# Gate and up products of a routed expert layer: one 128-column weight block, or two 64-column tiles

## The chip, the cores and the metric

The kernel runs on one core of a Trainium2 chip. The core has a matrix engine (TensorE, called PE in the profile), a vector engine (DVE), a scalar engine (ACT), GpSimd (POOL), a queue engine (SP), and sixteen DMA engines that bring data from main memory. The metric is the device time of one execution in microseconds; the median of three runs stands for a kernel. The profile lists a matmul twice: the loading of the stationary operand into the array (LDWEIGHTS, in the rows called PEld) and the streaming of the moving operand through it (MATMUL, called PE).

## The reference

The program is one step of a two-layer network on 640 tokens (128 prompt and 512 sample tokens) of width 1024. Layer 0 mixes the tokens by a bidirectional mLSTM, layer 1 by a bidirectional gated DeltaNet. After each mixer comes a mixture of 16 experts in which the experts choose tokens, and this is the part that is changed:

```python
aff = jax.nn.softmax((x @ w_router).astype(jnp.float32), -1)
gsel, idx = lax.top_k(jnp.swapaxes(aff, 1, 2), cap)
xs = x[bidx, idx]
hdn = jax.nn.silu(jnp.einsum('becd,edf->becf', xs, w_gate)) * jnp.einsum('becd,edf->becf', xs, w_up)
out = jnp.einsum('becf,efd->becd', hdn, w_down) * gsel[..., None].astype(x.dtype)
return jnp.zeros_like(x).at[bidx, idx].add(out)
```

Each expert takes 64 sample tokens and 16 prompt tokens, 80 in all. Its gate, up and down weights are 1024 by 1024 numbers each, in float32: 12 MB for one expert, of which there are 32 in the two layers.

## The kernel before

The work of each engine is written out by hand in program order, and semaphores tie the engines together; no planner decides anything. PE goes through the two layers one after the other: the modulation vectors, the projections, the scan of the mixer, the output projection (`mixer_tail`), and then `experts`.

An expert `e` has six weight halves of 2 MB, held in six slots: two halves each of gate, up and down, every half being 1024 rows by 512 columns. In the slots a row index is split into 8 blocks of 128 (`kt`) that lie on the 128 partitions. The loads of the next expert into a slot start when PE has finished the slot's products of the current expert: PE increments `moe_used`, SP (line 334) or ACT (line 681) waits for that and issues the load, and PE waits on `land[j]` for it before it uses the slot again.

On PE an expert has three stages. `hidden` (lines 1196 to 1206) forms the gate and up products. For each of the four halves `j` it goes through four blocks of 128 output features (`fb`) and for each through the eight blocks of the contraction (`kt`): the stationary operand is a 128 by 128 block of the weights, the moving operand is the block `kt` of the expert's tokens, 80 columns (`xsT`). The result, 128 features by 80 tokens, is accumulated over `kt` in bank `j` of PSUM at columns `fb*80`. That is 4 x 4 x 8 = 128 matmuls. `turn` (line 1193) transposes the tokens of the next expert, with eight matmuls. `down` (line 1215) has the 80 hidden columns as the stationary operand and 512 columns of the weights as the moving operand, 16 matmuls.

The operands are float32, and the trace holds two passes, each with a load and a streaming, for a float32 matmul of the program (a transpose has one). So an expert's 128 matmuls of `hidden` stand as 256 LDWEIGHTS and 256 MATMUL in the rows, its 16 of `down` as 32. "A pass" in this text is one load with its streaming.

ACT evaluates a tanh on the gate bank (line 687), and DVE makes the hidden values out of it (lines 1745 and 1748); `down` waits for the second half of these. DVE also scales and shifts the tokens of the next expert after the transposes, GpSimd gathers them and adds the finished rows of an expert to the output in memory. Expert 0, 1, 14 and 15 are written out, the others run in a loop whose body has two experts.

In the scan of layer 1 there is a place that the prediction reads too: lines 1088 and 1103 are matmuls of a 64 by 64 stationary block on one half of the partitions with 64 moving columns, which write to one half of the PSUM partitions.

Of the kernel before, what the change touches and what calls it, by code (L numbers as in the profile page):

```python
# [24 lines left out]
P = 128  # L25
D = 1024
KT = D // P
# [6 lines left out]
CAP = CAPS + CAPP  # L34
# [19 lines left out]
def backbone(nc, a):  # L54
# [3 lines left out]
    def S(name):  # L58
        if name not in sems:
            sems[name] = ctx.enter_context(nc.semaphore(name))  # L60
        return sems[name]
# [11 lines left out]
    with ctx:  # L73
        PS = ctx.enter_context(nc.psum_tensor("ps", [P, 8, HC], F32))
# [13 lines left out]
        slot = [s.rearrange("p (k n) -> p k n", k=KT) for s in SL]  # L88
# [48 lines left out]
        xsT = [wk[:, q * 640:(q + 1) * 640].rearrange("p (k c) -> p k c", k=KT) for q in range(2)]  # L137
# [55 lines left out]
        def moe_base(L, j):  # L193

            return ((L + 1) * sum(mix_slot(k) == j for k in range(MIX)) if j < 3 else 0) + L * EX
# [537 lines left out]
        def _(pe):  # L733
            mm = nc.tensor.matmul
# [433 lines left out]
            def gate_rows(first, bank, sem):  # L1168

                for c in range(2):  # L1170
                    for j in range(2):
                        for b in range(4):
                            ins = mm(PS[:, bank + 2 * c + j, b * P:(b + 1) * P],
                                     modT[:, first + 4 * j + b, c:c + 1].broadcast_to([P, P]), ident, start=True, stop=True)
                        ins.then_inc(sem, 1)

            def experts(L):
                pe.wait_ge(S("aff"), L * PER["aff"] + 1)
                tr(PS[0:EX, 2, 0:P], aff[:, 0, :], ident)
                for t in range(1, NT):  # L1180
                    ins = tr(PS[0:EX, 1, (t - 1) * P:t * P], aff[:, t, :], ident)
                ins.then_inc(S("afft"), 1)
                pe.wait_ge(S("topk"), L * PER["topk"] + 1)
                tr(PS[0:CAP, 3, 0:EX], vals[:, :], ident[0:EX, 0:EX])
                tr(PS[0:CAP, 3, EX:2 * EX], idf[:, :], ident[0:EX, 0:EX]).then_inc(S("selt"), 1)
                pe.wait_ge(S("sel"), L * PER["sel"] + 2)

                def turn(e, q, first):
                    pe.wait_ge(S("gathered"), L * PER["gathered"] + e * 16 + 16)
                    if not first:  # L1190
                        pe.wait_ge(S("xs_in"), L * PER["xs_in"] + e)
                    for kt in range(KT):
                        ins = tr(PS[:, 6 + kt // 4, (kt % 4) * CAP:(kt % 4 + 1) * CAP], xs[q][0:CAP, kt * P:(kt + 1) * P], ident[0:CAP, 0:CAP])
                    ins.then_inc(S("xs_turned"), 1)

                def hidden(e, q, first):
                    pe.wait_ge(S("xs_in"), L * PER["xs_in"] + e + 1)
                    for j in range(4):
                        pe.wait_ge(land[j], e * 16 + (16 * moe_base(L, j) + 16))
                        if not first:  # L1200
                            pe.wait_ge(S("hidden"), L * PER["hidden"] + e * 2 + (j // 2 - 1))
                        for fb in range(4):
                            for kt in range(KT):
                                ins = mm(PS[:, j, fb * CAP:(fb + 1) * CAP], slot[j][:, kt, fb * P:(fb + 1) * P],  # L1204
                                         xsT[q][:, kt, :], start=(kt == 0), stop=(kt == KT - 1))
                        ins.then_inc(S("moe_used"), 1)

                def down(e, q, first):
                    pe.wait_ge(S("hidden"), L * PER["hidden"] + e * 2 + 2)
                    for j in range(2):  # L1210
                        pe.wait_ge(land[4 + j], e * 16 + (16 * moe_base(L, 4 + j) + 16))
                        if not first:
                            pe.wait_ge(S("o_ready"), L * PER["o_ready"] + e * 2 + (j - 1))
                        for ft in range(KT):
                            ins = mm(PS[0:CAP, 4 + j, :], hdT[:, ft, :], slot[4 + j][:, ft, :],  # L1215
                                     start=(ft == 0), stop=(ft == KT - 1))
                        ins.then_inc(S("moe_used"), 1)

                def keep_clock(n):


                    for _ in range(n):
                        mm(PS[:, 4, :], ident, hT[:, 0, 0:HC], start=True, stop=True)

                keep_clock(5)
                turn(0, 0, True)
                keep_clock(3)
                hidden(0, 0, True)
                turn(1, 1, False)
                down(0, 0, True)  # L1230
                hidden(1, 1, False)
                turn(2, 0, False)
                down(1, 1, False)
                with pe.Fori(1, EX // 2 - 1) as i:
                    for q in range(2):
                        e = i * 2 + q
                        hidden(e, q, False)
                        turn(i * 2 + (q + 1), 1 - q, False)
                        down(e, q, False)
                hidden(EX - 2, 0, False)  # L1240
                turn(EX - 1, 1, False)
                down(EX - 2, 0, False)
                hidden(EX - 1, 1, False)
                down(EX - 1, 1, False)
                pe.wait_ge(S("hidden"), L * PER["hidden"] + 2 * EX)
                gate_rows(40, 0, S("g2b"))
# [601 lines left out]
```

## Time and profile before

| | |
|---|---|
| time, median of 3 runs (lowest to highest) | 3254.94 us (3253.11 to 3256.28) |
| span of the profiled execution, first to last instruction | 3254.3 us |
| PE busy with streaming, over the span | 3039.7 us (93%) |
| PE busy with weight loads (PEld) | 2229.6 us (69%) |
| DVE, ACT, POOL busy | 963.2, 577.3, 96.0 us |
| moved by DMA | 545.50 MB |

The profiled execution has no time of its own beside its span; the median of the runs is 0.64 us above the span. Durations of single instructions in the rows are longer than their distance from one to the next, because loads and streamings are pipelined: what a pass costs in a long row of them is the length of the group, less the duration of its last instruction, divided by the number of steps. All times below are in us from the span's start, unless they are marked ns.

### The profile page before, as it was taken

How to read it: one execution, taken by the hardware profiler on the slowest of the kernel's cores; microseconds unless marked ns; L12 is line 12 of the kernel's file. 1: busy time of each engine (PE TensorE's matmuls, PEld its weight loads, DVE VectorE, ACT ScalarE, POOL GpSimd, SP SyncE). 2: the span in 40 equal slices, each digit the busy share in tenths (PEclk: the TensorE clock that was granted, in tenths of full speed). 3: DMA queues.
4: the chain of work that ended last, by engine and by line, in shares of the span. 5: the costliest groups of instructions: out<-in, count | busy, mean ns of one | idle time of the engine just before them, and what ended most of it. 6: DMA issues, size and time to landing. Idle time of an engine off the chain costs nothing.

```text
span 3254.3 us, 43264 instructions
## 1 busy us (share of the span) xinstructions
PE 3039.7 (93%) x18405; PEld 2229.6 (69%) x18405; DVE 963.2 (30%) x2408; ACT 577.3 (18%) x1297; POOL 96.0 (3%) x145
## 2 busy tenths in 40 slices
PE   6999999797999999997999989999986999999994
PEld 1465479745887777771456459999944888777773
DVE  1100136643001000102177536666645010001002
ACT  3100111240000000003167212222242000000002
POOL 0000000000000000000000000000000000000000
PEclk9899998897999999998999999999997999999997
DMA  8411100217999999957411100000016899999992
GB/s 281 154 52 52 45 1 1 65 62 270 312 311 303 303 309 308 306 183 271 155 52 52 39 0 1 1 2 1 1 65 224 279 314 304 307 305 307 306 310 87
DMA packets 276365, 545.50 MB, mean 168 GB/s; under 512 B 15233, under 2 KB 23817, under 8 KB 276233
## 3 DMA queue, kind: packets, MB, share of 16 engines
q1 hardware_dynamic: 175049, 328.64, 29.4%
q10 hardware_dynamic: 93600, 188.75, 16.6%
q0 software_dynamic: 7584, 26.22, 3.2%
q8 instruction: 99, 1.62, 0.2%
q14 instruction: 33, 0.27, 0.0%
HBM read 517.89 MB, written 25.70 MB: 167 GB/s over the span
## 4 chain that ended last, share of the span: by engine, by line
PE 88%; DVE 6%; ACT 3%; DMA 2%; issue 1%; SPq 0%; DVEq 0%; POOL 0%; ACTq 0%
PE ps L1204 28%; PE ps L1215 14%; PE ps L803 8%; PE ps L813 6%; PE ps L760 5%; PE ps L1139 3%; PE ps L1101 3%; PE ps L804 2%; PE ps L1083 2%; PE ps L880 1%; PE ps L1115 1%; PE ps L791 1%; PE ps L950 1%; PE ps L966 1%; ACT L424 1%; ACT L423 1%
## 5 line engine op out<-in xcount | busy, mean ns | idle before, releaser
L1204 PEld LDWEIGHTS ps<-wk,slots 128*128 128x128 f32 x6144 | 691.1, 192 | 16.5 <-issue 16.0
L1204 PE MATMUL ps<-wk,slots 128*128 128x80 f32 x6144 | 689.9, 275 | 0.0
L1215 PE MATMUL ps<-qkv,og 128*80 128x512 f32 x1024 | 446.7, 594 | 2.4 <-DVE og L1748 1.3
L1215 PEld LDWEIGHTS ps<-qkv,og 128*80 128x80 f32 x1024 | 151.0, 150 | 275.5 <-issue 268.0
L803 PE MATMUL ps<-hT,slots 128*128 128x512 f32 x640 | 334.0, 604 | 3.1 <-ACT hT L455 3.1
L1204 PE MATMUL ps<-wk,qkv 128*128 128x80 f32 x2048 | 233.9, 275 | 0.0
L1204 PEld LDWEIGHTS ps<-wk,qkv 128*128 128x128 f32 x2048 | 231.3, 192 | 0.0
L804 PEld LDWEIGHTS ps<-hT,slots 128*128 128x128 f32 x640 | 123.5, 193 | 156.6 <-issue 156.6
L813 PE MATMUL ps<-slots,hT 128*128 128x512 f32 x480 | 209.3, 596 | 0.0
L760 PE MATMUL ps<-slots,cnd 128*2 128x512 f32 x384 | 172.0, 602 | 35.1 <-DVE x L1776 24.1
L1724 DVE COPY idc<-idT 80x1 uint32 (+1 forms) x32 | 4.8, 149 | 612.8 <-DMA moe_d<-og,idc 612.7
L813 PEld LDWEIGHTS ps<-slots,hT 128*128 128x128 f32 x480 | 91.8, 192 | 111.9 <-issue 111.6
L693 ACT ACTIVATE og<-ps,gsc 80x512 f32<-80x512 f32 x64 | 43.7, 683 | 657.8 <-PE ps L1215 657.8
L687 ACT ACTIVATE wk<-ps 128x320 f32<-128x320 f32 x64 | 28.0, 437 | 717.8 <-PE ps L1204 717.8
L1139 PE MATMUL ps<-slots,qkv 128*128 128x512 f32 x320 | 141.2, 600 | 8.0 <-DMA slots<-in_w_out_dram 5.7
L760 PEld LDWEIGHTS ps<-slots,cnd 128*2 128x2 f32 x384 | 31.2, 86 | 156.2 <-issue 155.8
L1748 DVE SCALAR_TENSOR_TENSOR og<-wk,ps 128x320 f32<-128x320 f32 x64 | 31.2, 487 | 327.1 <-PE ps L1204 327.1
L804 PE MATMUL ps<-hT,slots 128*128 128x128 f32 x640 | 124.1, 276 | 0.0
L1139 PEld LDWEIGHTS ps<-slots,qkv 128*128 128x128 f32 x320 | 60.8, 193 | 81.5 <-issue 81.5
L1745 DVE SCALAR_TENSOR_TENSOR wk<-wk,ps 128x320 f32<-128x320 f32 x64 | 31.2, 487 | 284.1 <-ACT wk L687 284.1
L1486 DVE SCALAR_TENSOR_TENSOR wk<-wk,vecT 128x128 f32<-128x128 f32 x192 | 105.9, 552 | 6.8
L803 PEld LDWEIGHTS ps<-hT,slots 128*128 128x128 f32 x640 | 99.9, 195 | 4.0 <-ACT hT L455 3.5
(261 smaller groups left out, 3228.5 us busy)
## 6 DMA issues: line engine op xcount, KB each, us to landing
slots<-in_w_gate_dram ACTq DMA_DIRECT2D x60, 2048.0 KB, 9.2
qkv<-in_w_down_dram SPq DMA_DIRECT2D x34, 2048.0 KB, 9.8
slots<-in_w_up_dram SPq DMA_DIRECT2D x32, 2048.0 KB, 10.2
qkv<-in_w_up_dram SPq DMA_DIRECT2D x32, 2048.0 KB, 7.8
qkv<-in_w_down_dram ACTq DMA_DIRECT2D x30, 2048.0 KB, 7.8
slots<-in_w_ada_dram SPq DMA_DIRECT2D x24, 2048.0 KB, 8.1
slots<-in_w_in_dram SPq DMA_DIRECT2D x16, 2048.0 KB, 8.1
slots<-in_w_out_dram SPq DMA_DIRECT2D x4, 2048.0 KB, 16.2
```

Source lines behind the costliest of these rows:

```text
L423: link(A(dst, src, ACT.Ln, scale=scale, bias=epst[:, 0:1]))
L693: A(osb[q][0:CAP, hf * HC:(hf + 1) * HC], PS[0:CAP, 4 + hf, :], ACT.Copy, scale=gsc[q][0:CAP, :]).then_inc(S("o_ready"), 1)
L760: ins = mm(PS[0:2, n % 2, :], cnd[:, 1, kt:16:8], slot[j][:, kt, :], start=(kt == 0), stop=(kt == KT - 1))
L803: mm(PS[:, b, :], w, hT[:, kt, P:TOK], start=(kt == 0), stop=(kt == KT - 1))
L804: ins = mm(PS[:, b + 1, 0:P], w, hT[:, kt, 0:P], start=(kt == 0), stop=(kt == KT - 1))
L813: ins = mm(PS[:, 2 * (i % n), :], hT[:, kt, t * P:(t + 1) * P], slot[sl][:, kt, :], start=(kt == 0), stop=(kt == KT - 1))
L1083: ins = mm(pack(four(PS[:, bx, :])[:, :, 0:64], l)[:, h], B["CM"][l % 2][:, h, :], cols1(B["D"][:, h, :], l, d), start=True, stop=True)
L1101: ins = mm(hb(2 * p + l % 2, h, 64), B["DT"][:, h, :], B["X"][:, h, :], start=True, stop=True)
L1139: ins = mm(PS[:, 6 + j, :], yT[:, kt, t * P:(t + 1) * P], slot[j][:, kt, :], start=(kt == 0), stop=(kt == KT - 1))
L1204: ins = mm(PS[:, j, fb * CAP:(fb + 1) * CAP], slot[j][:, kt, fb * P:(fb + 1) * P], xsT[q][:, kt, :], start=(kt == 0), stop=(kt == KT - 1))
L1215: ins = mm(PS[0:CAP, 4 + j, :], hdT[:, ft, :], slot[4 + j][:, ft, :], start=(ft == 0), stop=(ft == KT - 1))
L1486: ins = V.scalar_tensor_tensor(o_, s, w, o_, ALU.mult, ALU.add)
```

## The change

The innermost matmul of `hidden` becomes two. Each takes 64 of the 128 columns of the same weight block, streams the same 80 token columns, and writes its own half of the PSUM partitions, 0 to 63 or 64 to 127, at the same columns of the same bank. The two follow each other inside the loop over `kt`, so neighbouring matmuls alternate between the two halves of the array's columns. The results lie where they lay before; the number of matmuls in `hidden` goes from 128 to 256 for one expert, and from 4096 to 8192 for the program. The semaphore is incremented by the last of them, as before. On PE the order of the stages stays, and on the other engines no instruction is changed.

```diff
                         for fb in range(4):
                             for kt in range(KT):
-                                ins = mm(PS[:, j, fb * CAP:(fb + 1) * CAP], slot[j][:, kt, fb * P:(fb + 1) * P],
-                                         xsT[q][:, kt, :], start=(kt == 0), stop=(kt == KT - 1))
+                                for s in range(2):
+                                    c = fb * P + 64 * s
+                                    ins = mm(PS[64 * s:64 * s + 64, j, fb * CAP:(fb + 1) * CAP], slot[j][:, kt, c:c + 64],
+                                             xsT[q][:, kt, :], start=(kt == 0), stop=(kt == KT - 1))
                         ins.then_inc(S("moe_used"), 1)
```

## Rows read from the trace of the kernel before

**Rows 1.** The page: chain that ended last, and costliest groups (busy us, mean ns).

```profile
PE 88%; DVE 6%; ACT 3%; DMA 2%; issue 1%; SPq 0%; DVEq 0%; POOL 0%; ACTq 0%
PE ps L1204 28%; PE ps L1215 14%; PE ps L803 8%; PE ps L813 6%; PE ps L760 5%; PE ps L1139 3%; PE ps L1101 3%; PE ps L804 2%; PE ps L1083 2%; PE ps L880 1%; PE ps L1115 1%; PE ps L791 1%; PE ps L950 1%; PE ps L966 1%; ACT L424 1%; ACT L423 1%
...
L1204 PEld LDWEIGHTS ps<-wk,slots 128*128 128x128 f32 x6144 | 691.1, 192 | 16.5 <-issue 16.0
L1204 PE MATMUL ps<-wk,slots 128*128 128x80 f32 x6144 | 689.9, 275 | 0.0
...
L1204 PE MATMUL ps<-wk,qkv 128*128 128x80 f32 x2048 | 233.9, 275 | 0.0
L1204 PEld LDWEIGHTS ps<-wk,qkv 128*128 128x128 f32 x2048 | 231.3, 192 | 0.0
```

**Rows 2.** The chain in order of time, one expert of layer 0: start, length, what.

```profile
1019.77 0.56 PE ps L1193 x8
1020.33 0.03 issue
1020.35 13.96 PE ps L1215 x32
1034.31 28.54 PE ps L1204 x256
```

**Rows 3.** Timeline, 128-column loads: start, length, engine, line, shapes, count [idle before].

```profile
3015.80 7.23 PEld L1204 LDWEIGHTS ps<-wk,qkv 128*128 128x128 f32 x64
...
721.72 3.65 PEld L1145 LDWEIGHTS ps<-wrt,hT 128*128 128x128 f32 x32
```

**Rows 4.** Timeline, PE and PEld around the 64-column matmuls of layer 1.

```profile
1972.53 1.14 PE L1088 MATMUL ps<-slots 64*64 64x64 f32 x16
1973.60 0.65 PE L1006 MATMUL ps<-c,qkv 128*128 128x128 f32 x4
1974.09 1.06 PE L1008 MATMUL ps<-qkv 128*128 128x128 f32 x8
1975.08 1.14 PE L1103 MATMUL ps<-slots,wk 64*64 64x64 f32 x16
...
1975.08 1.00 PEld L1103 LDWEIGHTS ps<-slots,wk 64*64 64x64 f32 x16
```

**Rows 5.** Durations of these loads and streamings (min/median/max ns).

```profile
L1103 PEld LDWEIGHTS ps<-slots,wk x160: 129/135/135, 1975.1 to 2357.1; 64*64 64x64 f32 x160
L1103 PE MATMUL ps<-slots,wk x160: 218/218/267, 1975.1 to 2357.2; 64*64 64x64 f32 x160
L1193 PE MATMUL ps<-c,og x256: 230/232/236, 772.3 to 3152.7; 80*128 80x80 f32 x128
```

**Rows 6.** Timeline, streaming of 80 columns in the transposes, and the loads beside it.

```profile
1019.61 0.72 PE L1193 MATMUL ps<-c,og 80*128 80x80 f32 x8
...
1019.50 0.67 PEld L1193 LDWEIGHTS ps<-c,og 80*128 80x128 f32 x8
```

**Rows 7.** Windows: length, busy of PE, PEld, DVE, ACT, POOL, granted clock, DMA share, GB/s.

```profile
781.00:1441.00 660.00, 659.44 (x4563) 523.65 (x4563) 61.93 (x180) 34.05 (x61) 40.15 (x58) 1.00 0.89 301
1000.00:1043.07 43.07, 43.04 (x299) 33.99 (x297) 4.10 (x12) 2.24 (x4) 2.75 (x4) 1.00 0.91 307
740.00:760.00 20.00, 2.40 (x11) 1.56 (x10) 16.32 (x40) 0.27 (x1) 0.00 (x0) 0.50 1.05 387
```

## The prediction

> **What bounds the kernel now.** I read the page first: its chain puts 88% of the span on PE, and the line that changes, 1204, alone holds 28%; the groups give it 8192 loads and as many streamings, busy 922 us (691.1 and 231.3) and 924 us [rows 1]. The chain in order of time then shows a whole expert: 0.56 us of transposes, 13.96 of `down` and 28.54 of `hidden`, 43.07 us in all, with 0.03 us that is not PE [rows 2]. So inside an expert nothing but PE ends last, and each nanosecond on a pass of line 1204 is 8192 ns in the time. The windows say how far the next resource is: in such an expert the DMA share is 0.91 at 307 GB/s, and with PE nearly idle ahead of the experts it reached 387 GB/s [rows 7].
>
> What sets the pace of `hidden`? 64 loads of 128 columns take 7.23 us, so one follows another after (7.23 - 0.192) / 63 = 0.1117 us [rows 1, 3]. The router's matmuls load blocks of the same size and stream 16 columns instead of 80; theirs come every (3.65 - 0.19) / 31 = 0.1116 us [rows 3]. The distance doesn't depend on what is streamed, so the load sets it. The 80-column streaming can be read where the load is shorter, in the transposes: (0.72 - 0.232) / 7 = 0.0697 us [rows 5, 6]. A pass of line 1204 is thus a 112 ns load with a 70 ns streaming beneath it, and about 42 ns in which the array waits for weights.
>
> **The change, part by part.** It removes 8192 passes with a load of 128 columns and adds 16384 with a load of 64. Nothing else is added: no wait, no DMA, no instruction on DVE, ACT, POOL or SP.
>
> A 64-column load: the nearest rows are the 64 by 64 matmuls of line 1103, 16 loads in 1.00 us, (1.00 - 0.135) / 15 = 57.7 ns [rows 4, 5]. The row's rounding allows 57.3 to 58.0. They stream 64 columns, in less than that. That is a little over half of 112: 2 x 57.7 = 115.4 against 111.7 ns. So if loads go one after another and set the pace, splitting costs 115.4 - 111.7 = 3.7 ns for each old pass, up to 4.3 with the rounding: 8192 x 3.7 to 4.3 ns = 30 to 35 us. I take the upper end, 58.0 ns a load, since a group's length also carries a short first step.
>
> The streaming: two halves of 80 columns each, 2 x 69.7 = 139.4 ns for each old pass if they too go one after another. This is more than the two loads; PE would be bound by streaming, at 139.4 - 111.7 = 27.7 ns more for each old pass, 8192 x 27.7 = 227 us. If the halves of the array can stream at the same time, the streaming stays hidden. No row of this kernel shows neighbouring matmuls in different column halves: the sixteen passes of line 1103 all go to the same half, one after another.
>
> Between these two there is a middle case. A float32 matmul is two passes, so the order is two passes to the lower half, two to the upper. If a load has to wait until the stream ahead of it has begun, as in one undivided array, then of every two passes one shows its stream and one its load: 57.7 + 69.7 = 127.4 ns for each old pass, 15.7 more, 129 us.
>
> And from the other side: if both the loads and the streams of the two halves run side by side, an old pass costs one 80-column stream, 69.7 ns. `hidden` goes from 28.54 to 256 x 0.0697 = 17.8 us, and an expert's PE work to 17.8 + 0.56 + 13.96 = 32.4 us. Then DMA ends last: 43.07 us at 307 GB/s are 13.2 MB [rows 7], which take 34.2 us at 387 GB/s, or 43.07 x 0.91 / 1.05 = 37.3 us by the shares. 32 experts x (43.07 - 34.2 to 37.3) is a gain of 185 to 284 us.
>
> So the unknown runs from about -284 to +227 us, and the sign hangs on whether two weight loads go in parallel. Every row shows loads strictly one behind another on PEld, and the 128-column load is already as fast for its columns as the 64-column one. I take the loads as serial. For streams I take overlap between the halves: they use separate columns and separate PSUM partitions, and what a half waits for is only its own weights. That sets 116 ns, the value nearest to the rows of lines 1204 and 1103.
>
> The Trainium skill, page TensorEngine Tiling (Array Packing), section Tiling Modes, Key Properties, says that different tiles can execute weight loads and matmuls in parallel. No run here shows two tiles in turn, so the trace neither bears it out nor denies it; by this rule taken whole, the time would be that of the first rival.
>
> The switch of shape. Where 128-column matmuls are followed by 64-column ones, the first load is not pulled ahead. The last stream of line 1008 starts at 1974.09 + 1.06 - 0.275 = 1974.875 (its duration taken as line 1204's 275 ns [rows 1]), and line 1103 starts at 1975.08, 205 ns later, where the eight passes before stood (1.06 - 0.275) / 7 = 112 ns apart [rows 4]. On the way out, line 1088's last stream starts at 1972.53 + 1.14 - 0.218 = 1973.452 and line 1006 at 1973.60, 148 ns later instead of 58 [rows 4, 5]. That is 93 + 90 ns, and the first pass after it has its load uncovered, some 50 ns each. The new `hidden` is entered and left once for each expert: 32 x (93 + 90 + 2 x 40 to 50) ns = 8 to 9 us. It may be nothing, if a 64-column tile on all 128 rows needs no switch.
>
> The sum: 35 + 8 = 43 us on the chain, 3254.3 + 43 = 3297.3 for the span; the median of the runs stands 0.64 above the span now, so 3298. Nothing is late next: slots come free some 1.3 us later in an expert, and the loads into them had room, since PE waited 0.03 us in a period and not for DMA [rows 2]. The tanh and the products on DVE follow the end of a half as now.
>
> **The rivals.**
> *Both parallel (faster).* Loads and streams of the two halves overlap, and DMA bounds the experts: 2971 to 3070, middle 3020. For it: the halves share no column. Against it: the rows show loads only in sequence, and two of them at once would need twice the weight bytes a nanosecond that any row shows. It decides from the point where an old pass falls below 111 ns.
> *Streams serial (slower by much).* The streaming unit takes one matmul at a time, as every row does; 3254.9 + 227 + 9 = 3491. For it: line 1193 and all others, where streams never overlap. Against it: nothing but that the rows are all of one tile.
> *Half overlapped.* 3254.9 + 129 + 9 = 3393.
> *Load and stream of neighbours not overlapped at all.* 57.7 + 69.7 = 127.4 ns for each new pass, 254.8 for an old one, 143 more: 8192 x 143 = 1172 us, 4430. The row against it is that today's loads run beneath the streams. The Trainium skill, page TensorE: Matmul & The Clock Gate, section Part 3: Packing small matmuls, The mechanism, says that a weight load overlaps matmuls in flight only when its row group differs, and here both halves use all rows. The trace disagrees: the loads and streams of line 1204 share all rows and do overlap.
> *It does nothing.* Two half loads join without a gap, no switch is paid: within 6 us of 3254.9.
>
> **How the numbers follow.** Forecast, loads serial and streams hidden: 0.33, with its own range 3280 to 3312. Streams serial 0.26, half overlapped 0.11, both parallel 0.21, nothing overlapped 0.05, no change 0.04. Slower by over 0.2% (6.5 us, about what a measurement of this kernel can tell from no change): 0.33 + 0.26 + 0.11 + 0.05 = 0.75; faster 0.21; within it 0.04. The range should leave out 2 in 10: the 4430 case goes, the better half of the parallel case, and the edge of the serial one: 3000 to 3500.
>
> **What would show it.** The group of the new line holds 16384 loads of about 135 ns; 32 experts by a period. Right: an old pair every 115 to 117 ns, `hidden` at 29.5 us in the chain, PE at its end as now, clock at 1.00. Streams serial: a new pass every 70 ns, `hidden` at 35.7 us, PEld with idle time between loads. Parallel: loads less than 50 ns apart, and the chain or the waits of `hidden` name DMA. Wrong altogether: a granted clock under 1.00 inside `hidden`, or waits of PE for its instructions, which double in number.

## The result, and the profile after

The changed kernel takes 3117.54 us (median of 4 runs, 3112.63 to 3123.05) against 3254.03 us for the kernel before: 0.9579 of its time, 95% interval 0.9564 to 0.9594. It is 136 us faster. The prediction said 3298 us, slower, with a range of 3000 to 3500: the time lies inside the range, but on the other side of the time before.

The page of the changed kernel, the engines, the instruction queue and the chain (line 1204 is now 1206, and 1215 is 1217):

```profile
PE 2752.9 (88%) x26597; PEld 1914.8 (61%) x26597; DVE 963.2 (31%) x2408; ACT 576.8 (18%) x1297; POOL 95.8 (3%) x145
...
q8 instruction: 228, 3.74, 0.5%
...
PE 83%; DVE 6%; issue 6%; ACT 3%; DMA 2%; SPq 0%; DVEq 0%; POOL 0%; ACTq 0%
PE ps L1206 20%; PE ps L1217 14%; PE ps L803 9%; PE ps L813 7%; PE ps L760 5%; PE ps L1139 4%; PE ps L1101 3%; PE ps L804 2%; PE ps L1083 2%; PE ps L880 2%; PE ps L1115 1%; PE ps L966 1%; PE ps L962 1%; PE ps L950 1%; PE ps L791 1%
...
L1206 PE MATMUL ps<-wk,slots 128*64 128x80 f32 x12288 | 451.1, 234 | 84.6 <-issue 84.6
L1206 PEld LDWEIGHTS ps<-wk,slots 128*64 128x64 f32 x12288 | 436.5, 138 | 119.5 <-issue 118.0
...
L1206 PE MATMUL ps<-wk,qkv 128*64 128x80 f32 x4096 | 173.1, 247 | 67.2 <-issue 67.2
```

Two things stand against [rows 1]. The changed line streams 16384 passes in 451.1 + 173.1 = 624 us, where the old line took 924 us for half as many. And "issue", time in which PE waits for nothing that the profile shows, has gone from 1% of the chain to 6% of 3119 us, 187 us. The chain in order of time shows both in one expert (start, length, what); the answer to [rows 2]:

```profile
1008.10 4.64 PE ps L1206 x127
1012.75 1.90 issue
1014.64 4.64 PE ps L1206 x127
1019.29 1.44 issue
1020.73 4.59 PE ps L1206 x127
1025.31 2.83 issue
1028.14 5.33 PE ps L1206 x101
1033.47 0.70 PE ps L1193 x8
1034.17 13.84 PE ps L1217 x32
```

Inside a stretch a pass comes every (4.64 - 0.234) / 126 = 35.0 ns, 70 ns for an old block instead of 112: one 80-column stream, as in [rows 6], for both halves together. But after every 128 passes, that is 64 matmuls of the program, PE stands still for 1.4 to 2.8 us. A stretch with its gap takes 6.1 to 7.4 us.

What it waits for is in the DMA queues. The same 400 us inside the loop of layer 0, before and after (queue, kind: packets, MB, share):

```profile
q8 instruction: 2, 0.03, 0.0%
```

```profile
q8 instruction: 55, 0.90, 0.9%
```

The first is the kernel before: its two packets come at 918 and 932 us, at the start of the loop, and from there to 1388 us it fetches none. The second is the changed kernel, which fetches a packet of 16 KB (0.90 MB / 55) every 7.3 us on average. In the expert shown, packets have arrived at 1006.84, 1013.21, 1019.23 and 1026.78 us, and PE starts again 1.3 to 1.5 us after each; over the whole program all 92 such waits of line 1206 end 1.2 to 1.6 us after the arrival of a packet. The body of PE's loop, two experts, went from 304 matmuls to 560.

### The profile page after: what moved, and what is told of

It reads as the page before. It is cut to its first block, busy times and chain, and to the rows that moved or that the text cites. A ratio compares the mean times of both kernels' runs of the same rounds, so it can differ in the third digit from the quotient of the medians.

```text
span 3119.4 us, 59648 instructions
## 1 busy us (share of the span) xinstructions
PE 2752.9 (88%) x26597; PEld 1914.8 (61%) x26597; DVE 963.2 (31%) x2408; ACT 576.8 (18%) x1297; POOL 95.8 (3%) x145
## 4 chain that ended last, share of the span: by engine, by line
PE 83%; DVE 6%; issue 6%; ACT 3%; DMA 2%; SPq 0%; DVEq 0%; POOL 0%; ACTq 0%
PE ps L1206 20%; PE ps L1217 14%; PE ps L803 9%; PE ps L813 7%; PE ps L760 5%; PE ps L1139 4%; PE ps L1101 3%; PE ps L804 2%; PE ps L1083 2%; PE ps L880 2%; PE ps L1115 1%; PE ps L966 1%; PE ps L962 1%; PE ps L950 1%; PE ps L791 1%
## 5 line engine op out<-in xcount | busy, mean ns | idle before, releaser
L1206 PE MATMUL ps<-wk,slots 128*64 128x80 f32 x12288 | 451.1, 234 | 84.6 <-issue 84.6
L1206 PEld LDWEIGHTS ps<-wk,slots 128*64 128x64 f32 x12288 | 436.5, 138 | 119.5 <-issue 118.0
L1217 PE MATMUL ps<-qkv,og 128*80 128x512 f32 x1024 | 453.6, 601 | 2.2 <-DVE og L1750 1.3
L1206 PE MATMUL ps<-wk,qkv 128*64 128x80 f32 x4096 | 173.1, 247 | 67.2 <-issue 67.2
L1206 PEld LDWEIGHTS ps<-wk,qkv 128*64 128x64 f32 x4096 | 165.2, 148 | 71.7 <-issue 71.7
L1101 PE MATMUL ps<-wk,slots 128*128 128x64 f32 x800 | 98.7, 277 | 2.6 <-DVE wk L1620 2.6
```

The lines of the kernel that those rows point to most:

```text
L1101: ins = mm(hb(2 * p + l % 2, h, 64), B["DT"][:, h, :], B["X"][:, h, :], start=True, stop=True)
L1206: ins = mm(PS[64 * s:64 * s + 64, j, fb * CAP:(fb + 1) * CAP], slot[j][:, kt, c:c + 64], xsT[q][:, kt, :], start=(kt == 0), stop=(kt == KT ...
```

## The experiments

The theory after this was: neighbouring matmuls in the two halves load and stream side by side; the gaps are waits for instructions, because the longer body no longer stays on the chip, and the packets come late. Rivals were that a 64-column block is quicker in itself; that the gaps are weight loads; that the array pauses by itself.

**The alternation taken away.** The loop over the two halves goes outside the loop over `kt`.

```diff
-                            for kt in range(KT):
-                                for s in range(2):
+                            for s in range(2):
+                                for kt in range(KT):
```

> The loop over the two halves is put outside the loop over kt: the same 64-column matmuls, but sixteen passes in a row go to one half of the columns before the other half gets its sixteen. Theory (neighbouring matmuls in different halves load and stream side by side): now only the hand-over overlaps, so a pass costs its own 70 ns streaming, an old block 139 ns; hidden 35.7 us for an expert, no waiting for instructions since 64 matmuls last 8.9 us, time about 3254 + 227 + 9 = 3490 us. Rival (64-column blocks are quicker in themselves, in whichever order): 3117 us as in the changed kernel.

Measured 3260.82 us, 1.0016 of the time of before (1.0005 to 1.0026). The gain is gone, so it comes from the alternation, not from the width of the block; but the loss that was expected did not come either. The chain:

```profile
1016.71 13.83 PE ps L1217 x32
1030.54 29.05 PE ps L1206 x512
1059.60 0.70 PE ps L1193 x8
```

A pass takes 29.05 / 512 = 56.7 ns, between 35 and 70. In the start times of single passes most distances (9385 of 16352) are 69 or 70 ns, and nearly all others alternate between 5 to 13 and 56 to 64: some three passes of each sixteen run beside the first ones for the other half. So PE seems to begin with the other half while a few passes of the first still wait. There are no gaps, with 51 packets in the same 400 us and the weights moving at 307 GB/s: 64 matmuls now last 7.3 us.

```profile
q8 instruction: 51, 0.84, 0.8%
```

**One expert in the loop body.** For this the gathered tokens and the turned tokens have one buffer each, and the gather waits for the turn before it.

```diff
-        xs = [og[:, q * D:(q + 1) * D] for q in range(2)]
+        xs = [og[:, 0:D] for q in range(2)]
...
-        xsT = [wk[:, q * 640:(q + 1) * 640].rearrange("p (k c) -> p k c", k=KT) for q in range(2)]
+        xsT = [wk[:, 0:640].rearrange("p (k c) -> p k c", k=KT) for q in range(2)]
...
-                    if not first:
-                        pool.wait_ge(S("xs_turned"), L * PER["xs_turned"] + e - 1)
+                    if e is not 0:
+                        pool.wait_ge(S("xs_turned"), L * PER["xs_turned"] + e)
...
-                with pe.Fori(1, EX // 2 - 1) as i:
-                    for q in range(2):
-                        e = i * 2 + q
-                        hidden(e, q, False)
-                        turn(i * 2 + (q + 1), 1 - q, False)
-                        down(e, q, False)
-                hidden(EX - 2, 0, False)
-                turn(EX - 1, 1, False)
-                down(EX - 2, 0, False)
+                with pe.Fori(2, EX - 1) as e:
+                    hidden(e, 0, False)
+                    turn(e + 1, 0, False)
+                    down(e, 0, False)
```

> The changed kernel, with PE's loop body holding one expert instead of two, so that it has fewer instructions than the body of the kernel before (280 matmuls against 304); for this the gathered and the turned tokens have one buffer instead of two. Theory A (PE waits for its instructions: the body of two experts no longer stays on the chip and is fetched again in every iteration): the instruction queue falls silent inside the loop as before, the 1.4 to 2.8 us gaps in hidden go, an expert takes 33.2 us of PE or what the weight loads allow, 34 to 37 us; time 2990 to 3070 us. Theory B (the gaps are the weight loads): still 3110 to 3120 us. Theory C (the array pauses by itself after every 64 alternating matmuls): still 3110 to 3120 us, with gaps after every 128 passes.

Measured 2996.22 us, 0.9197 of before (0.9182 to 0.9213), inside what theory A gave. The queue of instructions has no packet at all in the 400 us window, and in the chain of the loop the gaps of `hidden` are gone; what ends last there now is a load of weights:

```profile
1027.63 4.67 PE ps L1206 x128
...
1032.45 30.43 DMA qkv<-in_w_up_dram
1062.88 0.04 issue
```

From one such wait to the next are 35.3 us for an expert. The window over that stretch (columns as in [rows 7]) shows DMA at 375 GB/s, near the 387 that [rows 7] had with PE nearly idle:

```profile
1027.60:1062.90 35.30, 32.71 (x552) 23.16 (x552) 4.59 (x13) 2.62 (x5) 2.75 (x4) 1.00 1.05 375
```

This kernel is the fastest that computes the whole. Theories B and C fall with it: the same weights and the same passes, and no gaps in the loop. Around the loop, in experts 0, 1, 2 and 15, whose instructions come from outside the loop or for the first time, some gaps stay (waits of PE: us, times, longest):

```profile
PE ps L1206 <- DMA qkv<-in_w_up_dram: 26.7, 15, 2.6
...
PE ps L1206 <- issue: 22.8, 16, 2.7
```

**The same loop without tiles.** The edit above (single buffers, one expert in the loop body) in the kernel before.

> The kernel before with the same one-expert body and single buffers, without the tiles. Control: PE paces the experts at 43.07 us either way; all theories 3254 us within 7. Above 3262 the single buffers cost something themselves.

Measured 3256.11 us, 0.9998 (0.9988 to 1.0009). The body and the single buffers are worth nothing by themselves; they are worth something only to a PE that runs faster.

**A long body without tiles.**

```diff
-                with pe.Fori(1, EX // 2 - 1) as i:
-                    for q in range(2):
-                        e = i * 2 + q
+                with pe.Fori(0, 3) as i:
+                    for n in range(4):
+                        q = n % 2
...
```

> The kernel before with four experts in PE's loop body (608 matmuls, more than the 560 of the changed kernel's body), no tiles. Theory A: the instruction queue runs through the whole loop, a 16 KB packet in about 14 us, but 64 matmuls at 112 ns a pass last 14.3 us, longer than a fetch takes to come (some 6.3 us from packet to packet in the changed kernel), so nothing is lost: 3254 us within 10. If a fetch stops PE whatever its pace (1.4 to 2.8 us for each of some 9 packets in two experts): 3254 + 12 x 2 x 8 x 2 = about 3400 us at most, over 3300 in any case.

Measured 3259.56 us, 1.0012 (1.0001 to 1.0022). The queue shows 27 packets in the 400 us, one in 14.8 us, and the chain has `hidden` at 28.54 us as before:

```profile
1028.91 28.54 PE ps L1204 x256
1057.45 0.56 PE ps L1193 x8
```

So fetching costs next to nothing here (4 us, 0.1%); it costs when PE uses up 64 matmuls faster than a packet comes.

**No weight loads.** The changed kernel, in which experts 1 to 15 of a layer load nothing and wait for no load. It leaves out the right weights of these experts; its line 1204 is the changed one, and `turn` and `down` are 1191 and 1215.

```diff
...
-                with sp.Fori(1, EX) as e:
-                    expert_loads(e, False)
...
-                        if not last:
+                        if False:
                             act.dma_start(slot[j], w_expert(L, e + 1, j)).then_inc(land[j], 16)
...
-                        pe.wait_ge(land[j], e * 16 + (16 * moe_base(L, j) + 16))
+                        pe.wait_ge(land[j], 16 * moe_base(L, j) + 16)
...
```

> The changed kernel (two experts in the loop body) without the weight loads of experts 1 to 15 of each layer: all experts use expert 0's weights, the DMA engines are nearly free. Theory A1 (an instruction packet is late because it queues behind the weight transfers): the gaps after every 128 passes go, an expert takes the 32.6 us of its PE work, 43.07 - 32.6 = 10.5 us less than before, 30 x 10.5 = 314 us less: about 2935 us. Theory A2 (a packet is asked for too late whatever the DMA does): the gaps stay at 1.4 to 2.8 us and the time near 3115 us.

Measured 2913.97 us, 0.8952 (0.8926 to 0.8978). Over the program it fetches the same 228 packets as the changed kernel, and the chain has no gap:

```profile
q8 instruction: 228, 3.74, 0.5%
```

```profile
1003.18 17.86 PE ps L1204 x512
1021.04 0.70 PE ps L1191 x8
1021.75 13.85 PE ps L1215 x32
```

The instructions are late only beside the weights: theory A1. In `hidden` of this expert packets start 3.8 to 4.1 us apart, and PE takes 4.5 us for 128 passes; in the expert of the changed kernel shown above they start 6.0 to 7.5 us apart. A packet itself takes about 1 us in both kernels, so the delay lies ahead of its transfer; that it queues there behind weight transfers, as A1 has it, is argued and not shown. An expert is 32.41 us, all of it PE.

**One expert in the body and no weight loads.** The two edits above together.

> The kernel with the one-expert body, also without the weight loads of experts 1 to 15. If weight loads now set its period (35.2 us, DMA share 1.00), PE falls to its own 17.9 + 0.8 + 13.9 = 32.6 us: 2996 - 30 x 2.6 = about 2918 us, with PE 100% busy in the loop. If something else set it, no change from 2996 us.

Measured 2912.62 us, 0.8948 (0.8922 to 0.8974), as in the run before. With the weights out of the way it no longer matters whether the body is fetched again. What holds the full kernel with this body at 2996 us, 84 us over PE's own 2913, therefore goes with the weight loads. Not all of it is waiting for weights: the waits above name the up weights for 26.7 us, and 22.8 us are instructions late beside the weights in the experts around the loop. The rest is not shown.

**Shorter streams.** The kernel of the run before, with 40 of the 80 tokens streamed.

```diff
-                                    ins = mm(PS[64 * s:64 * s + 64, j, fb * CAP:(fb + 1) * CAP], slot[j][:, kt, c:c + 64],
-                                             xsT[q][:, kt, :], start=(kt == 0), stop=(kt == KT - 1))
+                                    ins = mm(PS[64 * s:64 * s + 64, j, fb * CAP:fb * CAP + 40], slot[j][:, kt, c:c + 64],
+                                             xsT[q][:, kt, 0:40], start=(kt == 0), stop=(kt == KT - 1))
```

> As the run before, and each gate and up matmul streams only 40 of the 80 tokens (the other columns are left out). A pass now takes 34.9 ns, half of a 69.7 ns stream. If the streams set that and loads of the two halves go side by side, the pace falls to half of the 58 ns load, 29 ns: hidden 14.9 us, 30 x 3 = 90 us less than with 80 columns. If loads take turns at all (35 ns is their own pace), hidden stays at 17.9 us. If loads are free, it falls to 512 x 17.5 = 9 us.

Measured 2826.57 us, 0.8684 (0.8652 to 0.8716), 86 us less than with 80 columns. `hidden` in the chain:

```profile
985.60 15.06 PE ps L1204 x512
1000.66 0.70 PE ps L1191 x8
1001.36 13.85 PE ps L1215 x32
```

15.06 us / 512 = 29.4 ns a pass, half of the 58 ns that loads of this size take one behind another in a single half [rows 4, 5]. Each half is bound by its own loads, and the two halves do not disturb each other. With 80 columns each half is bound by its own streams, 17.86 / 512 = 34.9 ns, half of 69.7.

**Tiles for the gate halves alone.** The changed kernel, two experts in the body, with the up halves in one 128-column block. The edit is shown against the kernel before.

```diff
-                                ins = mm(PS[:, j, fb * CAP:(fb + 1) * CAP], slot[j][:, kt, fb * P:(fb + 1) * P],
-                                         xsT[q][:, kt, :], start=(kt == 0), stop=(kt == KT - 1))
+                                w = 64 if j in (0, 2) else P
+                                for s in range(P // w):
+                                    c = fb * P + w * s
+                                    ins = mm(PS[w * s:w * s + w, j, fb * CAP:(fb + 1) * CAP], slot[j][:, kt, c:c + w],
+                                             xsT[q][:, kt, :], start=(kt == 0), stop=(kt == KT - 1))
```

> The changed kernel (two experts in the body), but only the gate halves in 64-column tiles, the up halves in one 128-column block as before: 432 matmuls in the body. Theory A: an up half asks for instructions at a quarter of the pace of a gate half (64 passes at 112 ns for half a packet), so the fetch keeps up and the gaps go; hidden 2 x 4.5 + 2 x 7.15 = 23.3 us, expert 38 us, 32 x 5.1 = 163 us less than before: 3092 us, less than the full change. If the tiles' gain were simply halved: 3254 - 68 = 3186 us. Whether 432 matmuls stay on the chip shows in the instruction queue.

Measured 3107.52 us, 0.9547 (0.9519 to 0.9575). Half of the tiles give no less than all of them, since a slow half follows each quick one and leaves time for the next packet. The 432 matmuls of its body do not stay on the chip (46 packets in the 400 us window), and some gaps remain, here one of 1.06 us (lines 1207 and 1218 are `hidden` and `down`):

```profile
1006.54 1.25 PE ps L1207 x30
1007.79 1.06 issue
1008.85 22.85 PE ps L1207 x354
...
1046.25 23.76 PE ps L1207 x384
```

```profile
PE ps L1207 <- issue: 5.3, 6, 1.6
```

The gaps are not the 15 us over the expectation: the second line counts 5.3 us of them as waits. The last piece of the chain is an expert without a gap, and its `hidden` takes 23.76 us where 23.3 was expected. In 32 experts this is an estimate of 15 us. With it and the waits, and with 23.3 + 14.55 (`turn` and `down`) = 37.85 us for the rounded 38 of an expert, the sum of the expectation gives 3254 - 32 x 5.22 + 15 + 5 = 3107 us. The extra time lies where the halves change: a 64-column pass starts 205 ns after the last 128-column pass before it, as in [rows 4], where two 128-column passes stand 112 ns apart.

## Why the prediction was wrong

**What bounded the kernel before** was right: `hidden` was bound by 112 ns loads with 70 ns streams under them [rows 3, 6], and the gain came out of just those 42 ns.

**The step that failed is "I take the loads as serial".** All rows before showed loads one behind another, but all of them were loads into the same columns of the array; they could not tell what two halves do. They load side by side: a pass every 35.0 ns, where the forecast had 58 ns, and 29.4 ns where the streams were shortened. The half of the step that concerned streams ("I take overlap between the halves") was right. The rule that the prediction set against it holds: the Trainium skill, page TensorEngine Tiling (Array Packing), section Key Properties, says that tiles execute weight loads and matmuls in parallel, and the trace agrees with 35.0 ns for a pass against 57.7 for one load alone [rows 4, 5]. The sentence of the Trainium skill, page TensorE: Matmul & The Clock Gate, section Part 3: Packing small matmuls, The mechanism, that weight loads overlap with matmuls in flight only when the row group differs is once more not what is seen: the two halves use all rows, and loads still run beside streams.

**The rival that held, both parallel, was mis-sized**, at 2971 to 3070 us. Its pace for a block, 69.7 ns, was right to 0.3 ns (2 x 35.0), and its 32.4 us of PE work for an expert too: 32.41 us without weight loads. What it named as the next bound, the weight loads, is what the kernel with the one-expert body reached: 35.3 us an expert against the 34.2 to 37.3 worked out, and 2996 us. The changed kernel as written is held up before that, by its instructions. So 3117.5 us lies inside the range of the prediction by luck: it is above all that the parallel case allowed, through waits that the prediction gave no price, and below all the other cases. PE's own floor, the time without weight loads, is 2913 us; 3117.5 - 2913 = 204 us were given back. Waits of line 1206 with nothing shown as releaser hold 151.8 us of it (waits of PE: us, times, longest):

```profile
PE ps L1206 <- issue: 151.8, 92, 3.0
```

Another part is TensorE's clock. After two stops of PE, 1.75 and 2.21 us long, the granted clock was 0.89 in the next row, and `down`, 13.84 us elsewhere, took 15.54 (the chain, then the rows with the stops and with `down`, columns as in [rows 7]):

```profile
990.93 15.54 PE ps L1217 x32
```

```profile
980.00:990.00 10.00, 6.04 (x167) 5.72 (x163) 0.49 (x1) 0.44 (x1) 0.00 (x0) 1.00 1.04 362
991.00:1006.40 15.40, 15.40 (x33) 4.97 (x32) 1.88 (x6) 0.68 (x1) 0.00 (x0) 0.89 0.88 318
```

In the first row PE was busy for 6.04 of 10.00 us. The loss is 15.54 - 13.84 = 1.7 us. The trace has 18 such stretches at the lower level (1.2 GHz) inside the experts, which gives an estimate of 18 x 1.7 = 31 us. Waits and clock make 183 of the 204 us; the rest is not shown.

**"Nothing else is added"** was the second fault. The prediction counted no instruction bytes and named "waits of PE for its instructions" only as something that would prove it wrong, without a price. The page of before lists them, 99 packets in the whole span:

```profile
q8 instruction: 99, 1.62, 0.2%
```

The Trainium skill, page Runtime: NRT & Kernel Launch, section Instruction fetch mechanics, gives PE's instruction memory as 128 KiB, refilled in blocks of 16 KiB, and calls the cost of a refill mostly hidden. The trace agrees on the block (0.90 MB in 55 packets) and on a limit of this order: a body of 304 matmuls isn't fetched again, bodies of 432 and more are. At 64 matmuls a block, 432 are an estimate of 6.75 blocks of 16 KiB, 108 KiB, so a body can be fetched again that is smaller than the size the page gives. "Mostly hidden" holds at 14 and at 7.3 us a block beside the weights, and at 4.5 us a block only without them.

**The switch of shape** was put at 8 us and cost next to nothing. `turn`, which follows the tiles, takes 0.70 us instead of 0.56, but `down` takes 13.85 instead of 13.96 with 0.03 before it [rows 2]: 14.55 us in both kernels. The way in is small within `hidden`, 17.86 us for 512 x 34.85 ns (half of the 69.7 ns stream) = 17.84 us. The price was read from places between 64-column and 128-column blocks, and the kernel with tiles for the gate halves alone, which has such places inside `hidden`, does pay about 0.5 us an expert. In the changed kernel `hidden` is not broken up in this way.

## What to carry to other kernels

Where weight loads bound short matmuls, alternate between the two column halves: each half then loads and streams at its own pace, but only if neighbours in program order alternate (35 ns a pass; 57 with sixteen in a row to each half). Rows that show a resource serial are no evidence for two of it when all of them use the same one; give the parallel case more weight then. When matmuls are split, count the loop body as well: here a body that had to be fetched again was free at 112 ns a pass, and took back 204 of 341 us at 35 ns beside heavy weight traffic (and in the clock that fell behind it); a loop over one expert instead of two gave back 121 of them.

## What the runs showed of the hardware that was not expected

- Blocks of sixteen passes for one half already overlap with the next sixteen for the other: 56.7 ns a pass, where 69.7 had been expected.
- An instruction packet of 16 KB seems to hold the 64 float32 matmuls between two gaps, 128 passes. The loop fetches more packets than that: in the kernel with blocks of sixteen, the 400 us with 51 packets have 5121 passes, which would fill 40. Where the others come from is not shown.
- At 4.5 us a packet, instructions are late only beside weight traffic: the same 228 packets go with 204 us more at 334 GB/s in the loop than at 22 GB/s, where PE is busy throughout. The windows (columns as in [rows 7]) of the changed kernel and of the one without weight loads:

```profile
800.00:1350.00 550.00, 474.04 (x7654) 332.83 (x7652) 55.55 (x163) 31.35 (x56) 38.46 (x56) 0.98 0.97 334
```

```profile
900.00:1100.00 200.00, 200.00 (x3326) 140.41 (x3324) 24.54 (x72) 13.46 (x24) 16.45 (x24) 1.00 0.12 22
```
